# Expert blocks: the rows of block b+2 are turned ahead of the up projection of block b+1

## The reference

```
def moe(x2d, router_w, router_bias, exp_w1, exp_w3, exp_w2, shared_w1, shared_w3, shared_w2):
    ...                                  # each of 1152 tokens picks 8 of 64 experts, with weights
    def expert_block(args):              # a block: up to 128 tokens of one expert
        tok, e = args
        xb = x2d[tok]
        hb = jax.nn.silu(xb @ exp_w1[e]) * (xb @ exp_w3[e])
        return hb @ exp_w2[e]
    yb = lax.map(expert_block, (slot_tok.reshape(NB, MOE_BLOCK), block_expert))
    routed = jax.ops.segment_sum(yb.reshape(P, D) * slot_w[:, None].astype(x2d.dtype), slot_tok, num_segments=N)
    shared = (jax.nn.silu(x2d @ shared_w1) * (x2d @ shared_w3)) @ shared_w2
    return routed + shared
```

## Time and profile before

| | us |
|---|---|
| median of 3 runs | 2127.23 (2119.42 to 2136.78) |
| the profiled execution | 2126.18, of which the span of the trace 2124.4 |
| PE busy | 1924.1 (91%) |
| DVE busy | 1268.9 (60%) |
| ACT busy | 1073.9 (51%) |
| POOL busy | 774.5 (36%) |
| DMA | 391.15 MB, 184 GB/s over the span |

### The profile page before, as it was taken

One profiled execution on the slowest core, in us unless ns is written; L12 is line 12 of the kernel. 1 busy time (PEld: TensorE's weight loads), 2 busy tenths in 40 slices (PEclk: granted clock), 3 DMA queues, 4 the chain that ended last, 5 costly groups with the idle time before them and its releaser, 6 DMA issues. The chain is left out here.

```text
span 2124.4 us, 31754 instructions
## 1 busy us (share of the span) xinstructions
PE 1924.1 (91%) x8869; PEld 1347.6 (63%) x8870; DVE 1268.9 (60%) x1853; ACT 1073.9 (51%) x1530; POOL 774.5 (36%) x764
## 2 busy tenths in 40 slices
PE   4787998999998798599999999999999999999990
PEld 2344444999896454466777776676777777676760
DVE  3376447432777589775666566556556656566556
ACT  3354545432234111456666666566666666566652
POOL 4211000000013034533646543445666663345560
PEclk8899999999999999699999999999999999999995
DMA  8742100332103323437966997865688788887854
GB/s 264 235 137 102 62 20 20 119 120 70 11 1 139 125 90 120 149 124 265 309 206 195 323 347 240 284 182 151 190 259 255 240 272 285 295 291 263 281 146 178
DMA packets 119388, 391.15 MB, mean 184 GB/s; under 512 B 28574, under 2 KB 53150, under 8 KB 94366
## 3 DMA queue, kind: packets, MB, share of 16 engines
q1 hardware_dynamic: 72908, 271.53, 34.8%
q0 software_dynamic: 46128, 118.81, 21.9%
q10 hardware_dynamic: 290, 0.02, 0.0%
HBM read 347.08 MB, written 81.45 MB: 202 GB/s over the span
## 5 line engine op out<-in xcount | busy, mean ns | idle before, releaser
L2088 DVE TENSOR_TENSOR wupl<-big,wuph 128x2048 fp32r<-128x2048 f32 x234 | 525.8, 2289 | 454.2 <-ACT wuph L2026 454.1
L2026 ACT ACTIVATE wuph<-big 128x2048 fp32r (+1 forms) x234 | 435.8, 1917 | 12.1 <-issue 6.9
L1951 PE MATMUL bank<-w,hT 128*128 (+1 forms) x920 | 414.3, 593 | 0.0
L1930 PE MATMUL bank<-wuph,xTh 128*128 128x512 f32 x928 | 373.6, 403 | 5.4 <-DVE xTl L2097 5.1
L1930 PE MATMUL bank<-wuph,xTl 128*128 128x512 f32 x928 | 364.9, 393 | 0.0
L1930 PE MATMUL bank<-wupl,xTh 128*128 128x512 f32 x928 | 363.7, 392 | 0.0
L1864 POOL DMA_INDIRECT yacc_scratch<-y,idx_s x106 | 207.3, 1955 | 388.6 <-issue 319.6
L1951 PEld LDWEIGHTS bank<-w,hT 128*128 128x128 f32 x920 | 166.3, 191 | 165.3 <-issue 165.3
L1830 POOL COPY idx_s<-shared 128x1 int32 x106 | 209.4, 1975 | 1.8 <-issue 0.9
L2016 ACT ACTIVATE y<-bank 128x512 f32<-128x512 f32 x115 | 68.8, 598 | 279.1 <-PE bank L1951 253.4
L1930 PEld LDWEIGHTS bank<-wuph,xTh 128*128 128x128 f32 x928 | 176.5, 190 | 41.0 <-issue 7.6
(11 more groups left out here) (361 smaller groups left out, 2703.4 us busy)
## 6 DMA issues: line engine op xcount, KB each, us to landing
big<-in_exp_w SPq DMA_DIRECT2D x128, 1024.0 KB, 8.6
w<-in_exp_w SPq DMA_DIRECT2D x64, 1024.0 KB, 8.3
wada<-in_w_ada POOLq DMA_DIRECT2D x16, 1024.0 KB, 6.3
wg<-in_w_in SPq DMA_DIRECT2D x14, 1024.0 KB, 5.4
wada<-in_w_ada SPq DMA_DIRECT2D x4, 2048.0 KB, 12.0
big<-in_w_in SPq DMA_DIRECT2D x8, 1024.0 KB, 5.4
x<-x_scratch SPq DMA_DIRECT2D x9, 512.0 KB, 4.2
x_scratch<-x SPq DMA_DIRECT2D x9, 512.0 KB, 3.1
```

Of the source, the lines that this page charges most:

```text
L1930: mm = pe.matmul(b_up[j][:, :], x[:, k, :], w[:, :, k, :], start=(k == 0 and i == 0), stop=(k == KT - 1 and i == 2))
L1951: mm = pe.matmul(b_down[half][:, :], hT[:, i, :], w2[:, at, i, half * 512:(half + 1) * 512].rearrange("p s n -> p (s n)"), start=(i == 0), ...
L2026: act.activation(part13(wup[j][0], half), raw13(e % WSLOT, half), ACT.Copy).then_inc(w_high, 1)
L2088: dve.tensor_tensor(part13(wup[j][1], half), raw13(e % WSLOT, half), part13(wup[j][0], half).bitcast(F32), ALU.subtract).then_inc(w_low, 1)
```

## The change

In both places where PE's list is written (the shared blocks and the loop of the routed ones), `turn` of block b+2 moves from behind `up` of block b+1 to before it. `down` of block b then follows `up` directly. No other engine's list is touched.

```
--- before.py
+++ after.py
@@ -1974,8 +1974,8 @@
             up(0, 0)
             for b in range(NSH):
                 turn_h(b, b % 2)
+                turn(b + 2, b % 2)
                 up(b + 1, (b + 1) % 2)
-                turn(b + 2, b % 2)
                 down(b, b % 2)
                 if b == 1:
                     places()
@@ -1987,8 +1987,8 @@
                 for u in range(2):
                     b, j = r * 2 + (u + NSH), (u + NSH) % 2
                     turn_h(b, j)
+                    turn(r * 2 + (u + NSH + 2), j)
                     up(r * 2 + (u + NSH + 1), 1 - j)
-                    turn(r * 2 + (u + NSH + 2), j)
                     down(b, j, r * 2 + u)
```

## The result

| | before | changed |
|---|---|---|
| median, us (20 runs each) | 2125.59 | 2135.16 |
| lowest to highest | 2115.84 to 2136.78 | 2128.47 to 2148.59 |
| the profiled execution | 2126.18 | 2134.61 |

The changed kernel takes 1.0052 of the time of before (95% interval 1.0035 to 1.0068): slower by some 10 us (9.6 between the medians, 11 by that ratio), by less than 1%. Two executions far off the rest, 10962.49 us of the kernel with only the shared blocks changed and 2598.01 us of a before, are left out.

A forecast was written before the change was run, and what follows sets the result against it. The prediction took PE's own instructions, 10.04 us a block, to bound the expert stage. Waits and clock, 5.5 + 4.2 + 0 + 1.7 + 1 = 12.4 us, on 2126.2 gave 2138.6, with the median 2139.6: forecast 2139 us, range 2126 to 2156.

The forecast's parts named there:

- The start: Start of the routed blocks: PE idles before turning block 8, then block 9's gathered rows set the time; +5.5 us.
- the clock: New idle in the crowded stretch can bring PE's lower clock level once more, in one of three waiting blocks; +1.7 us.
- Point 1: PE's wait for the low part of the turned rows moves from up projection to turn, staying 5.1 us; cost 0.
- Point 2: An earlier turn only removes ACT's 0.51 us wait before its copies and lets no gather start earlier; 0.
- Point 3: Switches between kinds of matmul on PE: only up to down is new, bounded by +10 or -10 us; taken as 0.
- my rival on the other side: New handovers save 0.09 us of every block, 10 us of 115 blocks, giving 2128 us; chance 0.05.
- Point 4: PE's wait for gathered rows: spare falls from 8.3 to 2.7 us, costing at the start and in crowded stretches.
- the middle: Crowded stretch, gather landing at 1379.84 us: PE waits without the up projection as cover; +4.2 us.
- the late place: Gather issued at 1824.42 us: PE waits for its rows but no longer runs into late hb; about 0.
- near misses: An allowance for near misses elsewhere, beyond the places worked out; 1 us.
- The rival of many places: The scatter queue becomes the bound in many places; five waits at 7.3 us make 36 us, 2162 us; chance 0.22.
- The rival that the loop costs nothing: Late stretches don't answer as worked out, scatters may land at 7.7 us; only the start costs, 2132 us; chance 0.18.

The follow-up runs named there:

- the earlier load: Block 8's plainly loaded rows are asked for before the slot table is finished, against the changed kernel; 1.0049 of before.
- the plain store: The adding scatter replaced by a plain store of fixed rows: order of before 2115.06 us, 0.9941 of before; changed order 2118.81 us, 0.9976.
- the loop-only kernel: Only the loop of the routed blocks turns early, against the kernel before, the shared blocks keeping their order; 1.0046 of before.
- the two parts alone: Against the kernel before, the new order in the shared blocks only, 1.0029, and in the loop of the routed blocks only, 1.0046.

## Why the prediction was right

The forecast was 2139 us, +0.6%; measured 2135.16, +0.45% by the medians and +0.52% by the ratio. The prediction held that a change under 1% can't be told from none here; with 20 executions each it can (1.0035 to 1.0068). Step by step:

- **The start, +5.5 us.** Profiled +5.75, and +6.2 us in the kernel that changes only the shared blocks. Right in place, size and cause (the earlier load shows that the gathered rows of block 9 set it). One detail was off: I let the clock's loss vanish in the wait of block 9, but this wait didn't come. Before, those rows landed 19.4 us after the turn of h of block 6; PE, 1.77 us late, came to them 19.7 us after it, and its list shows no wait there. The end is the same, since the two terms replace each other.
- **Point 1, the wait for the low part,** changed its owner and cost nothing, as forecast. It didn't keep its size: 5.1 us before, 2.5 us after without the wait at block 1 that both kernels have. With the same order the kernel with block 8's rows loaded earlier has 3.6 us, so I count no gain.
- **Point 2, ACT's wait of 0.51 us** went (the copy follows the silu with no gap) and brought nothing. Right.
- **Point 3, the handovers,** taken as 0 within 10 us either way. They gave 0.02 us a block, 2.1 us in 106 blocks. This is the one gain of the change, and a fifth of the price of my rival on the other side.
- **Point 4, the middle (+4.2), the late place (0), the clock (+1.7) and near misses (+1): 6.9 us in all.** The mechanism was right: the waits come in the crowded stretches, and they go in both orders with the plain store or with fewer bytes of weights. The sum is about right as well: by the estimate above the waits of the new order cost 6.7 us more, and 4.6 after the gain of point 3. But this agreement is in part luck, since the places were not right. I had read them from one execution, and it had lost 15.2 us in the loop where another one of the same order lost 6.6. The wait of 3.12 us of the earlier trace rows is no fixed point of the kernel, and in the changed profile the middle has four waits of 2.1 us and less.
- **The spare behind point 4 was misread.** I took the 8.3 us of one gather for the usual case, 2.7 after the move. The trace of before has a median of 10.4 us in the quiet stretch and 4.4 in the crowded one, and 20 gathers of the loop with less than the 5.57 us of the move. What is fixed is the distance of the move, and not the spare. So the term should have been built as a chance for each of these 20 gathers, not as one place with a price; the eleven waits of the loop-only kernel are of that kind. By the same mistake I gave near misses 1 us; that kernel paid 6.4 us for one.
- **Late, PE no longer runs into hb.** ACT's wait for the scatter queue at its copy of y was 21.5 us before and doesn't appear in the changed profile's list. Right in kind.
- **The rival of many places** (2162 us) priced each wait at 7.3 us; the eleven waits of the loop-only kernel average 1.4 us of idle, and the whole loss of its loop, with the clock and the other waits, is 24.3 / 11 = 2.2 us for each. It described the pattern better than my forecast did, and was about three times too dear. The rival that the loop costs nothing is refuted by 1.0046 (1.0024 to 1.0067).

What stays open: by the ratios the two parts alone sum to +16 us and the whole is +11; by the medians they sum to 11.5 and the whole is +9.6. The intervals allow both to be about 5 and 6. Whether a late start spares the loop something wasn't tested.

## What to carry to other kernels

A step that is moved forward costs nothing by itself on a busy engine, but its waits move with it: work out the spare of every awaited transfer before the move, and not of one (here 0 to 15 us, half of them under 7.9), subtract the distance (5.57 us), and count those that fall below nothing. Read the crowded stretches from several executions, since their place and depth differ between runs, while the distance doesn't. And before giving a queue's customer more room, look at who stands behind it: the gather put ahead of the scatter cost more than the wait that it removed.

## What the runs showed of the hardware that I had not expected

Loading half of the partitions, with a quarter of all bytes in the stretch gone, left the DMA engines as busy as before (0.84 for 0.85) and the kernel slower by 0.34%; loading fewer bytes over all partitions lowered the share to 0.77 and the time by 0.52%. And the order of the kinds of matmul has a small price of its own, 10.047 against 10.027 us for the same instructions.

A short idle can cost as much again in the clock, or nothing. The idle of 1.85 us at 960.03 in the kernel before left the granted clock at 1.00. This one, in the changed kernel, is as long, and the granted clock behind it was 0.50 from 1842.4 to 1845.4 us:

```profile
1839.07 0.39 PE L1937 MATMUL bank<-cst,hb 128*128 128x128 f32 x2
1841.33 1.18 PE L1917 MATMUL bank<-cst,xg 128*128 128x128 f32 x8 [1.87 <-DMA xg<-hn_scratch,idx_g]
...
1852.86 0.39 PE L1937 MATMUL bank<-cst,hb 128*128 128x128 f32 x2
```

The block took 13.79 us, 3.76 more than a quiet one: 1.87 of idle and 1.89 more, at the lower clock. Why the two differ stays open.
